# Projections of the odd mixer as three single passes of split operands, with x stored and reloaded

## The reference

```python
def odd_mixer(h, hc, w_in, pool_w, pool_scale, conv_w, conv_b, wa, ba, wx, bx, lam, need_ctx):
    z = h @ w_in
    ux, ug, up = jnp.split(z, CD_SPLITS, axis=-1)
    zc = hc @ (w_in if need_ctx else w_in[:, :LRU_W])
    xl = depthwise_conv(ux, conv_w, conv_b, LRU_PAD)
    ...
    for d, reverse in enumerate((False, True)):
        ...
        a_l, b_l = rglru_coeffs(xl, wa[d], ba[d], wx[d], bx[d], lam[d])
        h_lat = h_lat + linear_scan(a_l, b_l, h0, reverse)
    lat = [multiscale_pool(up, pool_w, pool_scale), h_lat.astype(ug.dtype) * jax.nn.gelu(ug)]
```

## Time and profile before

| | |
|---|---|
| median of the timed runs | 2317.36 us |
| the profiled execution | 2310.29 us, span 2308.5, mean granted TensorE clock 0.972 |
| busy in the span | PE 2140.2 (93%), DVE 990.2 (43%), ACT 764.8 (33%), POOL 237.4 (10%) |
| float32 products with `w_cd` (line 2814) | 448 records (two a matmul), 183.4 us |
| `odd_mixer` | from 1299.0 (first instructions of its block) to 1587.1 (DVE's last `gated`) |
| next load of SP, `w_o` | issued at 1587.58 |

### The profile page before, as it was taken

The page is one execution under the profiler, slowest core; times in us unless marked ns, Lnnn a source line. Parts: engine busy times, 40 slices in busy tenths (PEclk is TensorE's granted clock), DMA queues, the critical chain, the costliest instruction groups (busy, mean ns, idle before and its releaser), DMA issues. The chain is left out here.

```text
span 2308.5 us, 33768 instructions
## 1 busy us (share of the span) xinstructions
PE 2140.2 (93%) x14210; PEld 1198.9 (52%) x14210; DVE 990.2 (43%) x1511; ACT 764.8 (33%) x1163; POOL 237.4 (10%) x160
## 2 busy tenths in 40 slices
PE   7999998989997999999999889998987999998885
PEld 5788875546674555555555444444854333333221
DVE  6333226655335544435444453766543222222221
ACT  5411105554214544434444355565233010101000
POOL 0010000000000000000000302551000111111110
PEclk9999999999999999999999999999999999999998
DMA  9201108017708999999999711004339999999995
GB/s 355 65 28 37 37 19 355 1 35 258 264 10 313 409 410 428 426 427 426 426 426 426 270 56 40 19 18 146 146 106 371 392 396 403 407 409 412 412 413 183
DMA packets 142860, 587.43 MB, mean 254 GB/s; under 512 B 26004, under 2 KB 62576, under 8 KB 117488
## 3 DMA queue, kind: packets, MB, share of 16 engines
q1 hardware_dynamic: 116960, 516.48, 55.8%
q0 software_dynamic: 13568, 40.91, 5.5%
q10 hardware_dynamic: 12176, 27.81, 3.2%
HBM read 529.06 MB, written 63.18 MB: 257 GB/s over the span
## 5 line engine op out<-in xcount | busy, mean ns | idle before, releaser
L2260 PE MATMUL ph<-w,x_t 128*32 128x512 f32 x4288 | 482.3, 602 | 23.4 <-DMA w<-in_exp_w 23.3
L2260 PEld LDWEIGHTS ph<-w,x_t 128*32 128x32 f32 x4288 | 137.2, 111 | 314.7 <-issue 311.6
L2297 PE MATMUL py<-w,g_t 128*32 128x512 f32 x2144 | 245.0, 597 | 15.6 <-DMA w<-in_exp_w 14.5
L2515 DVE TENSOR_TENSOR hidden<-hidden,ph 64x512 f32<-64x512 f32 x68 | 73.8, 1085 | 386.9 <-ACT hidden L2430 386.0
L2430 ACT ACTIVATE hidden<-ph 64x512 f32<-64x512 f32 x68 | 40.2, 591 | 570.1 <-PE ph L2260 570.1
L2506 DVE TENSOR_TENSOR w_low<-w,w_high 128x1024 fp32r<-128x1024 f32 x156 | 180.6, 1220 | 12.5 <-ACT w_high L2416 12.4
L2814 PE MATMUL z<-hT,w_cd 128*128 128x512 f32 (+1 forms) x448 | 183.4, 567 | 0.0
L825 PE MATMUL z<-h_high,w_hi 128*128 128x512 f32 (+1 forms) x432 | 159.8, 370 | 3.9 <-DVE h_low L920 3.5
L2416 ACT ACTIVATE w_high<-w 128x1024 fp32r<-128x1024 f32 x156 | 152.1, 1048 | 19.1 <-PE ph L2270 15.2
L826 PE MATMUL z<-h_low,w_hi 128*128 128x512 f32 (+1 forms) x432 | 156.0, 361 | 0.0
L827 PE MATMUL z<-h_high,w_lo 128*128 128x512 f32 (+1 forms) x432 | 155.9, 361 | 0.0
(11 more groups left out here) (397 smaller groups left out, 3072.8 us busy)
## 6 DMA issues: line engine op xcount, KB each, us to landing
w<-in_exp_w SPq DMA_DIRECT2D x187, 2048.0 KB, 22.6
ada_raw<-in_ada_w SPq DMA_DIRECT2D x13, 2048.0 KB, 8.0
y_slots<-zero SPq DMA_DIRECT2D x29, 512.0 KB, 15.1
w<-in_ada_w SPq DMA_DIRECT2D x5, 2048.0 KB, 13.1
h_tokens<-h_rows ACTq DMA_DIRECT2D x18, 512.0 KB, 3.1
w_ab<-in_w_in_ab SPq DMA_DIRECT2D x14, 512.0 KB, 3.8
y_slots<-y_rows ACTq DMA_DIRECT2D x26, 256.0 KB, 10.7
y_slots<-y_rows ACTq DMA_DIRECT2D x52, 128.0 KB, 9.2
```

The costliest lines, as they stand in the source:

```text
L2260: ins = pe.matmul(ph[row:row + UNIT, :], xt[:, k, at:at + UNIT], up_of(place[u + n])[:, half, k, :], start=(k == 0), stop=(k == KT - 1))
L2297: ins = pe.matmul(py[bufs[i][0]][row:row + UNIT, :], gt[:, k, n * UNIT:(n + 1) * UNIT], down_of(place[u + n])[:, k, half * 512:(half + 1) ...
L2515: dve.tensor_tensor(hid[PAIR:P, :].rearrange("s (k q) -> s q k", k=FT), hid[0:PAIR, :].rearrange("s (q k) -> s q k", k=FT), ph[PAIR:P, :]. ...
```

## The change

The products with `w_cd` are made of split numbers: a high part, which is what is left when a float32 number is written as F32R, and a low part, the difference. Three single-pass matmuls (high x high, low w x high h, high w x low h) take the place of one float32 matmul. For it:

- ACT writes `h_hi` beside `hT`, each from the same input (`modulated`). `h_hi` lies in the place of `h_low` of the first layer, whose second half is now under `xT`; so x of chunks 0 and 1 is first stored to DRAM by SP (ACT waits for `s_keep`), and it is loaded back, 4 MB, when all units are done. POOL makes the low part, in the place of `hT`, per chunk and k.
- ACT makes the high part of each weight tile (`split(m)`), DVE the low part in the tile's own place (`w_rest(m)`). The weight ring has two slots and a third place for tile 2, which lies where later `lru_total`, the lanes' scratch and a pool buffer are; DVE's `under_root(0, 0)` and POOL's window sums of i=0 wait until unit 6 is done (`FIRST_READ`).
- The rings of gathered rows have four tiles (NB) for five, `lru_total` two rows for three; `gated(0)` comes earlier, in the turn of i=1.

```diff
@@ -2652,11 +2652,22 @@
             pool_at[n] = i
             pool_in[n - 1], pool_in[n] = 2 * i, 2 * i + 1
         NW = 3
-        NB = 5
+        NB = 4
+        before = {m: (m - 3 if m < 5 else m - 2) for m in range(NW, len(tiles))}
+        w_slot = [m if m < NW else (m - NW) % 2 for m in range(len(tiles))]
+        w_turn = [1 if m < NW else (m - NW) // 2 + 2 for m in range(len(tiles))]
+        split_at = {last_of[before[m]] + 1: m for m in before}
+        FIRST_READ = place["ug", 0, 1] + 1
         part = [range(at // P, (at + size) // P) for at, size in CHUNKS]
         with ExitStack() as ctx:
+            with ExitStack() as same_place:
+                h_lo = self.sb(same_place, "h_low_odd", [P, KT, TOK], F32R)
             hT = self.sb(ctx, "hT", [P, KT, TOK])
-            w = self.sb(ctx, "w_cd", [P, NW, KT, P])
+            h_hi = self.h_low
+            with ExitStack() as same_place:
+                w_lo = self.sb(same_place, "w_cd_low", [P, 2, KT, P], F32R)
+            w = self.sb(ctx, "w_cd", [P, 2, KT, P])
+            w_hi = self.sb(ctx, "w_cd_high", [P, 2, KT, P], F32R)
             gw = self.sb(ctx, "gate_w", [P, 2, 2, BR, P])
             pw = self.sb(ctx, "pool_weights", [P, BR, P])
             up = self.sb(ctx, "u_pad", [P, LRU_ROW])
@@ -2666,10 +2677,19 @@
                 ya = self.sb(same_place, "y_a", [P, NB, D])
                 yb = self.sb(same_place, "y_b", [P, NB, D])
             lanes = [[self.sb(ctx, f"lru{d}{n}", [P, L]) for n in range(3)] for d in range(2)]
+            kept = self.sb(ctx, "lru_total", [P, 2, SEQ])
+            total = [kept[:, i % 2, :] for i in range(BR - 1)] + [lanes[0][1][:, 0:SEQ]]
+            with ExitStack() as same_place:
+                w_third_lo = self.sb(same_place, "w_third_low", [P, KT, P], F32R)
+            with ExitStack() as same_place:
+                w_third = self.sb(same_place, "w_third", [P, KT, P])
             sqr = self.sb(ctx, "a_squared", [P, L])
-            kept = self.sb(ctx, "lru_total", [P, BR - 1, SEQ])
-            total = [kept[:, i, :] for i in range(BR - 1)] + [lanes[0][1][:, 0:SEQ]]
-            pp = [self.sb(ctx, f"pool{n}", [P, PAD + SEQ + PAD]) for n in range(2)]
+            pp = [self.sb(ctx, "pool0", [P, PAD + SEQ + PAD])]
+            with ExitStack() as same_place:
+                w_third_hi = self.sb(same_place, "w_third_high", [P, KT, P], F32R)
+            pp.append(self.sb(ctx, "pool1", [P, PAD + SEQ + PAD]))
+            w_raw, w_high, w_low = ([which[:, w_slot[m], :, :] if m != 2 else third[:] for m in range(len(tiles))]
+                                    for which, third in ((w, w_third), (w_hi, w_third_hi), (w_lo, w_third_lo)))
             z = [self.ps(ctx, f"z{i}", [P, 512]) for i in range(2)]
             pa, pxg = self.ps(ctx, "pa", [P, 3 * 512]), self.ps(ctx, "pxg", [P, 3 * 512])
             turned = [pa[:, 0:D], pxg[:, 0:D]]
@@ -2680,9 +2700,11 @@
                 self.sem(ctx, "o_" + n) for n in ("sum", "fwd", "gw", "pw", "zero", "z", "ux", "ug", "up", "cv", "pg", "r", "a", "q", "sqr",
                                                   "b", "h", "gu", "y", "pl", "pd", "pm", "pe", "ch"))
             s_ya, s_yb = ([self.sem(ctx, f"c_{n}{i}") for i in range(NB)] for n in ("ya", "yb"))
-            row = kept[:, 2, 0:512]
+            row = kept[:, 1, 512:1024]
             c_wa, c_wb, c_t, c_x, c_sq, c_rows, c_copy, c_sum, c_var, c_std, c_rstd, c_bc, c_n, c_h = (
                 self.sem(ctx, "c_" + n) for n in ("wa", "wb", "t", "xx", "sq", "rows", "copy", "sum", "var", "std", "rstd", "bc", "n", "h"))
+            s_wh, s_wl, c_hi, c_lo = (self.sem(ctx, "o_" + n) for n in ("wh", "wl", "hi", "lo"))
+            s_keep = self.sem(ctx, "o_keep")
             block = ctx.enter_context(nc.Block())
             W = self.i["w_in_cd"][0].rearrange("(k p) n -> p k n", p=P)
             both = ((0, 0, SEQ), (SEQ, GAP, CTX))
@@ -2707,9 +2729,9 @@
                 base = {"ux": 0, "ug": SC_W, "up": 2 * SC_W}
                 for m, (kind, i, parts) in enumerate(tiles):
                     if m >= NW:
-                        sp.wait_ge(s_z, last_of[m - NW] + 1)
+                        sp.wait_ge(s_z, last_of[before[m]] + 1)
                     at = base[kind] + i * P
-                    sp.dma_start(w[:, m % NW, :, :], W[:, :, at:at + P]).then_inc(s_w[m % NW], 16)
+                    sp.dma_start(w_raw[m], W[:, :, at:at + P]).then_inc(s_w[w_slot[m]], 16)
                     if m == len(early) - 1:
                         sp.wait_ge(s_zero, 1)
                         for d in range(2):
@@ -2718,6 +2740,14 @@
                                     sp.dma_start(gw[par * HD:(par + 1) * HD, d, gate, :, par * HD:(par + 1) * HD],
                                                  self.i[name][0, d, par::2, :, :].rearrange("i h j -> h i j")).then_inc(s_gw, 16)
                         sp.dma_start(pw[:], self.i["pool_w"][0].rearrange("g i j -> i g j")).then_inc(s_pw, 16)
+                        for c in range(2):
+                            sp.wait_ge(c_x, part[c][-1] + 1)
+                            here = slice(CHUNKS[c][0], sum(CHUNKS[c]))
+                            sp.dma_start(self.xs[:, :, here], self.xT[:, :, here]).then_inc(s_keep, 16)
+                            sp.wait_ge(s_keep, 16 * c + 16)
+                sp.wait_ge(s_z, len(unit))
+                sp.dma_start(self.xT[:, :, 0:SEQ], self.xs[:, :, 0:SEQ]).then_inc(s_keep, 16)
+                sp.wait_ge(s_keep, 48)
 
             @block.tensor
             def _(pe):
@@ -2804,15 +2834,19 @@
                         pe.wait_ge(s_gw, 16 * 8)
                         pe.wait_ge(s_pw, 16)
                     if c == 0:
-                        pe.wait_ge(s_w[m % NW], 16 * (m // NW + 1))
+                        pe.wait_ge(s_wl, m + 1)
                     if n >= 2:
                         wait_z_read(pe, n - 2)
                     at, size = CHUNKS[c]
                     for k in range(KT):
                         if kind == "ux" and i == 0:
-                            pe.wait_ge(c_h, KT * c + k + 1)
-                        ins = pe.matmul(z[n % 2][:, 0:size], w[:, m % NW, k, :], hT[:, k, at:at + size],
-                                        start=(k == 0), stop=(k == KT - 1))
+                            pe.wait_ge(c_hi, KT * c + k + 1)
+                        out = z[n % 2][:, 0:size]
+                        pe.matmul(out, w_high[m][:, k, :], h_hi[:, k, at:at + size], start=(k == 0), stop=False)
+                        pe.matmul(out, w_low[m][:, k, :], h_hi[:, k, at:at + size], start=False, stop=False)
+                        if kind == "ux" and i == 0:
+                            pe.wait_ge(c_lo, KT * c + k + 1)
+                        ins = pe.matmul(out, w_high[m][:, k, :], h_lo[:, k, at:at + size], start=False, stop=(k == KT - 1))
                         if k == KT - 1:
                             ins.then_inc(s_z, 1)
                         for what, which in between.get((n, k), ()):
@@ -2849,8 +2883,16 @@
                     of = int(at >= SEQ)
                     for k in ks:
                         act.wait_ge(c_n, KT * c + k + 1)
+                        if c < 2:
+                            act.wait_ge(s_keep, 16 * c + 16)
+                        act.activation(h_hi[:, k, at:at + size], hT[:, k, at:at + size], ACT.Identity, bias=self.mods[:, 1, 0, k, of:of + 1],
+                                       scale=self.gain[:, 1, 0, k, of:of + 1]).then_inc(c_hi, 1)
                         act.activation(hT[:, k, at:at + size], hT[:, k, at:at + size], ACT.Identity, bias=self.mods[:, 1, 0, k, of:of + 1],
                                        scale=self.gain[:, 1, 0, k, of:of + 1]).then_inc(c_h, 1)
+
+                def split(m):
+                    act.wait_ge(s_w[w_slot[m]], 16 * w_turn[m])
+                    act.activation(w_high[m], w_raw[m], ACT.Copy).then_inc(s_wh, 1)
 
                 def pool_out(i, c, n):
                     act.wait_ge(s_pm, 2 * i + c + 1)
@@ -2907,6 +2949,8 @@
                         act.activation(pp[0][:, PAD + at:PAD + at + size], z[n % 2][:], ACT.Copy).then_inc(s_up, 1)
 
                 act.activation(stat[:, 3, 0:1], self.c("ones", 1), ACT.Sqrt)
+                for m in range(NW):
+                    split(m)
                 scale(0)
                 scale(1)
                 for t in range(4):
@@ -2946,6 +2990,8 @@
                 for n, (m, i, kind, c) in enumerate(unit):
                     if n >= len(early):
                         evict(n)
+                    if n in split_at:
+                        split(split_at[n])
                     if n in pool_at:
                         pool_out(pool_at[n], 0, n - 1)
                         pool_out(pool_at[n], 1, n)
@@ -2996,6 +3042,12 @@
                     for k in ks:
                         dve.tensor_tensor(hT[:, k, at:at + size], self.xT[:, k, at:at + size], bc[:, 0:size], ALU.mult).then_inc(c_n, 1)
 
```

(24 more changed lines are left out.)

## The result

The changed kernel takes 2359.76 us, the median of 4 runs (2356.91 to 2363.16); the kernel before took 2316.36 beside it (4 runs). The ratio is 1.0188, with an interval of 1.0163 to 1.0214: slower, by 43 us. The forecast was 2354, with 2334 to 2370 as its range.

What follows compares the result with a forecast made beforehand. A loop through PE, ACT, POOL and DVE, not PE's projections, was taken to bound the middle of `odd_mixer`. 8 + 5.5 + 9 - 5 + 2.3 + 4 + 13.5 = +37 on 2317.4 gave 2354, range 2334 to 2370.

Steps and rivals of the forecast that it cites:

- T: Mark at the end of `conv(3)`, 1528.2 in the trace before the change; forecast 23.8 us later.
- The third tile: Start of the front: first transposes wait for the third weight tile's load, split and sum; +8 us, between 5 and 9.
- The save: Front: first `modulated` waits for the save of chunk 0 of x, slowed by gathers; +5.5 us, between 1 and 8.
- Passes and subtractions: Front, up to `conv(0)`: ACT's extra passes and POOL's subtractions, less shorter units; net +9 us, bounds 0 and 16.
- To the first product: From `conv(0)` to the product of i=0: shorter units 6 to 9 on the path; -5 us.
- The loop: Products of i=0 to i=2: `w_rest` on DVE, DVE and POOL stretching each other, low PE clock; +2.3 and +4 us.
- The tail: From the end of `conv(3)` to the stage's end: later last units, then waiting for x's 4 MB reload; +13.5 us.
- A: Rival, from `conv(0)` on: PE sets the pace after all; 2318, or 2310 without the front's first 8 us; chance 0.15.
- B: Rival, front: waits are covered, tile lands early, save takes 8 us; 2344, or 2340 with faster tail; chance 0.17.
- C: Rival: covers fail; POOL's subtractions stretch, tiles 5, 7, 9 split late, reload takes 16 us; 2368; chance 0.18.
- D: Rival, projection matmuls: the products are not single passes; given no chance.

Runs made afterwards that it cites:

- after_late_split: Changed kernel with the third weight tile's split and subtraction moved later, so the first `scale` and `added` don't wait for its load: 2351.38 us, ratio 1.0140.
- after_no_low_h: Changed kernel without the low part of h: no second ACT pass, no POOL subtractions, two matmul passes per step: 2334.29 us, ratio 1.0074.
- after_one_pass: Changed kernel with only one of the three matmul passes (high w x high h), all else unchanged: 2338.99 us, ratio 1.0086.
- after_kept_warm: Changed kernel with PE running idle matmuls in place of waiting for POOL ahead of the pooling products: 2351.96 us, ratio 1.0143.
- before_save_reload: Kernel before the change plus only the two saves of x, ACT's wait for them and the reload: 2338.06 us, ratio 1.0076.
- after_two_conv: Changed kernel with a second buffer for the convolved input, so `conv(i)` doesn't wait for POOL's multiply of (i-1, 1): 2355.09 us, ratio 1.0148.
- after_two_reloads: Changed kernel with x reloaded in two halves, the first once the last unit reading chunk 0 is done: 2354.75 us, ratio 1.0159.
- after_dve_full: Changed kernel with `hT` made by DVE, one `tensor_scalar` per k, and ACT writing only `h_hi`: 2354.89 us, ratio 1.0155.

## Why the prediction held, and where it was off

The chain was right, and the sum was 4 us low by the trace (+37 for +41.4). That it came so close is in part luck: five terms were too small by 8.8 us together, two too large by 4.3, and T came 0.4 us less late than the product of i=2. The first two lie outside the bounds that I gave them (5 to 9, and 1 to 8). By its terms:

1. **The third tile: +8 forecast, +10.8 measured** at the first `new_x`. The mechanism is the one told, and `after_late_split` shows it. The size came from one landing of 15.4 us; in the changed kernel it was 18.2, and in ten more executions with the same loads it lay between 14.8 and 18.3. A single landing beside gathers is a draw from some 3 us of spread, and the range for this step should have had it on both sides.
2. **The save: +5.5 forecast, +9.0 measured.** I took a value between the save alone (8.2 us) and equal turns of packets (14.5 from its issue at 1333 to 1347.5). Measured: 15.4, with 1040 packets on SP's queue and 967 on the gathers'. The Trainium skill (DMA: Bandwidth & Descriptors, Queues, rings and completion order) says that a DMA engine goes round its queues packet by packet. The trace agrees, with these counts, and by equal turns the sum would have been off by 2 instead of 4. The step that failed is the choice between two bounds; the row that showed the very same collision should have decided it.
3. **Passes and subtractions: +9 forecast, +9.8 measured** (61.3 us for 51.5). DVE stood idle for 12.8 us before the last statistics, ended by PE, and that is the front's chain: ACT's double passes, then PE's units. The bound of 0 is excluded by `after_no_low_h`, and `after_one_pass` shows that PE's passes are the smaller part. POOL's subtraction took 1.38 us, not 1.16, and still lay under ACT's 1.41 (two passes of 0.70).
4. **To the first product: -5 forecast, -4.6 measured.**
5. **The loop: +2.3 and +4 forecast, +0.4 and +5.3 measured.** The sum was right and the split was not. `w_rest` on DVE cost 0.9 us a turn for the 1.25 forecast: from `conv` to POOL's second multiply it is 14.2 us in both turns, for 13.3. The low clock lies in turn two, as forecast, with 1.8 us for 2.2, and `after_kept_warm` gains 1.8 us there and nothing in turn one. The mis-sized term is how far POOL's window sums and DVE's work stretch each other, +1.1 and +0.5 forecast: from the end of the multiply to the product it took 12.3 us for 13.0 in turn one (-0.7) and 17.9 for 15.4 in turn two (+2.5). `gated(0)`, for which the 1.1 stood, did not lengthen the sums; it paid itself instead, with 4.61 us where two of it alone take 1.3. In turn two 1.4 of the 2.5 us lie in POOL's two short additions (2.29 us for 0.89, at 1536.19). A scan of DVE and `w_rest(6)`, which I had priced at nothing, ran beside them; no run separates the two.
6. **The tail: +13.5 forecast, +11.2 measured**, 70.5 us from T for 59.4. `under_root(3,0)` began at T+19.0 (T+21 forecast), the last product was evicted at T+56.9 (T+59.4), and the reload took 13.7 us to `w_o` (13). So the exposed transfer was right and the chain ahead of it 2.5 us too long; `before_save_reload` gives 9.4 us for the transfer by itself.

The rivals: A, that PE sets the pace, is refuted by `after_one_pass`. B, that the front's waits are covered, is refuted by ACT's two waits of 12 us. C, failing covers, did not come true: the loads of tiles 3 to 11 never made PE wait in the loop, POOL's subtraction kept pace, and the reload landed in 13.3 us. From the first product on PE waited 0.3 us in all for a low part of a tile. D, products that are not single passes, is excluded: in the tail the evictions of two units of 512 tokens start 5.44 us apart (1607.25 and 1612.69), as forecast for 24 single passes.

What stays open: the ratios of `after_late_split`, `after_two_conv`, `after_two_reloads`, `after_dve_full` and `after_kept_warm` are known to some 3 parts in a thousand each, and their intervals overlap that of after. Their gains rest on the stretches of one trace each.

## What to carry over

When a change takes work from the busiest engine, follow the loop from one product to the next through every engine before counting the gain; where the loop doesn't pass through that work, even two thirds of it gone moves nothing. First cut the chain that sets the pace (a second buffer, and the sums ahead of a multiply that nobody waits for), and only then make the hidden work cheaper. Borrowing a place that has to be stored and reloaded has its price at both ends, and a transfer beside gathers is to be priced by the row that shows the two queues side by side.

## What the runs showed of the hardware

- A load of 512 KB took 14.8 to 18.3 us beside the gathers, for 3.8 in the even layer, and the first save of 2 MB 15.1 to 17.4 for 8.2. Saves issued earlier took longer (15.4 at 36.9 us from the start, 17.3 at 25.8); I put that down to more gathers beside them, which no run here separates.
- A reload of 4 MB took 13.3 us, one of 2 MB 8.7 at the same place: half the bytes took two thirds of the time.
- DVE and POOL held each other up. Two window sums of POOL took 5.23 us and the two `gated` beside them 4.61. Alone, such a sum took 1.92 and such a `gated` 0.69: two of each are 5.22, about what either engine needed, which fits two engines that take turns. The fit isn't exact, since POOL's first sum began 1.1 us before the first `gated`. The Trainium skill (SBUF — State Buffer, SBUF: two separate sides) says that of a DVE instruction with two inputs in SBUF and a GpSimd one that reads SBUF, the one that starts first holds the ports that they share for the whole instruction; the trace agrees, with these numbers.
- PE's first product after 7 us of waiting took 2.1 us for 1.0, at a granted clock of 0.50 (1.2 GHz), and the gates behind it 3.2 for 2.3; with idle matmuls in the wait it was 1.1, at 1.00 (2.4 GHz). The granted clock over the stretch from the first product to `w_o` was 0.89, for 0.98 before.
